# Causal mask as a TensorE product on the scores, softmax read from the bank, early scores, and a pool product beside the mixer's attention

## The reference, cut to what matters

```python
s = jnp.einsum('bqhd,bkhd->bhqk', q_blk, k, preferred_element_type=jnp.float32) * scale
if cum_t is not None:                      # forgetting attention (FoX)
    s = s + c_q[..., :, None] - cum_t[:, :, None, :]
s = jnp.where(k_pos[None, :] <= q_pos[:, None], s, NEG_INF)
p = jax.nn.softmax(s, axis=-1).astype(v.dtype)
return jnp.einsum('bhqk,bkhd->bqhd', p, v)
```

## Time and profile before

| | |
|---|---|
| median of 3 runs | 1812.03 us (1811.85 to 1817.65) |
| profiled execution | 1805.45 us, span 1803.7 us |
| busy: PE, DVE, ACT, POOL | 1641.2, 1204.0, 862.6, 56.5 us |
| mean granted TensorE clock | 0.936 of 2.4 GHz |
| chain that ended last | PE 71%, DVE 17%, ACT 5%, DMA 4% |
| layers, mixer, top-k and first table, second table end | to 716, to 917, to 1401, to 1788 us |

### The profile page before, as it was taken

The page is one execution under the profiler, slowest core; times in us unless marked ns, Lnnn a source line. Parts: engine busy times, 40 slices in busy tenths (PEclk is TensorE's granted clock), DMA queues, the critical chain, the costliest instruction groups (busy, mean ns, idle before and its releaser), DMA issues.

```text
span 1803.7 us, 30500 instructions
## 1 busy us (share of the span) xinstructions
PE 1641.2 (91%) x10734; PEld 1411.2 (78%) x10734; DVE 1204.0 (67%) x2585; ACT 862.6 (48%) x1380; POOL 56.5 (3%) x87
## 2 busy tenths in 40 slices
PE   6888898898989787998879999989999999999996
PEld 5666866796767665786769999989999777778885
DVE  3575556645655665544565899978878899975554
ACT  3654354344334553343334666656556344435543
POOL 1020100100000201000000000000000000000000
PEclk9999898899888898896889999999999999999998
DMA  6542452355425543551334445544444444455552
GB/s 232 179 164 105 146 190 91 140 172 178 140 71 177 180 141 143 189 191 66 117 130 174 140 166 183 187 142 161 163 160 145 159 164 163 163 186 192 201 188 93
DMA packets 40469, 282.96 MB, mean 157 GB/s; under 512 B 5297, under 2 KB 5441, under 8 KB 6865
## 3 DMA queue, kind: packets, MB, share of 16 engines
q1 hardware_dynamic: 37136, 267.13, 41.8%
q0 software_dynamic: 3264, 14.94, 2.4%
HBM read 279.94 MB, written 2.12 MB: 156 GB/s over the span
## 4 chain that ended last, share of the span: by engine, by line
PE 71%; DVE 17%; ACT 5%; DMA 4%; issue 2%; POOL 1%; DVEq 0%; ACTq 0%; SPq 0%; POOLq 0%
PE banks L566 19%; PE banks L567 18%; PE banks L568 18%; DVE w_lo L1147 4%; DMA raw<-stream 4%; PE banks L608 3%; PE banks L854 3%; PE banks L656 3%; PE banks L670 2%; ACT w_hi L912 1%; PE banks L628 1%; ACT scratch L977 1%; PE banks L682 1%; PE banks L681 1%; PE banks L680 1%
## 5 line engine op out<-in xcount | busy, mean ns | idle before, releaser
L1147 DVE TENSOR_TENSOR w_lo<-raw,w_hi 128x1024 fp32r<-128x1024 f32 x456 | 560.7, 1232 | 407.0 <-ACT w_hi L912 403.9
L912 ACT ACTIVATE w_hi<-raw 128x1024 fp32r<-128x1024 f32 x456 | 482.2, 1058 | 584.0 <-PE banks L568 501.5
L566 PE MATMUL banks<-w_hi,xT_hi 128*128 128x512 f32 (+2 forms) x1140 | 454.5, 399 | 20.3 <-DVE xT_lo L1179 16.2
L567 PE MATMUL banks<-w_lo,xT_hi 128*128 128x512 f32 (+2 forms) x1140 | 445.1, 390 | 0.0
L568 PE MATMUL banks<-w_hi,xT_lo 128*128 128x512 f32 (+2 forms) x1140 | 444.9, 390 | 0.0
L566 PE MATMUL banks<-xT_hi,w_hi 128*128 128x256 f32 x1360 | 394.5, 290 | 5.2 <-ACT xT_hi L958 1.5
L567 PE MATMUL banks<-xT_lo,w_hi 128*128 128x256 f32 x1360 | 388.4, 286 | 0.0
L568 PE MATMUL banks<-xT_hi,w_lo 128*128 128x256 f32 x1360 | 388.3, 286 | 0.0
L566 PEld LDWEIGHTS banks<-w_hi,xT_hi 128*128 128x128 f32 x1140 | 218.9, 192 | 66.4 <-ACT xT_hi L958 13.0
L566 PEld LDWEIGHTS banks<-xT_hi,w_hi 128*128 128x128 f32 x1360 | 264.9, 195 | 7.2 <-ACT arena L1077 2.6
L567 PEld LDWEIGHTS banks<-xT_lo,w_hi 128*128 128x128 f32 x1360 | 264.7, 195 | 0.0
(11 more groups left out here) (188 smaller groups left out, 1495.7 us busy)
## 6 DMA issues: line engine op xcount, KB each, us to landing
raw<-stream SPq DMA_DIRECT2D x252, 1024.0 KB, 4.8
arena<-ln_in POOLq DMA_DIRECT2D x4, 1024.0 KB, 5.0
arena<-mod_rows POOLq DMA_DIRECT2D x2, 1536.0 KB, 8.8
arena<-g_in POOLq DMA_DIRECT2D x3, 512.0 KB, 7.3
arena<-x_in SPq DMA_DIRECT2D x1, 1024.0 KB, 5.1
arena<-bands_in POOLq DMA_DIRECT2D x1, 1024.0 KB, 5.2
arena<-keys_in POOLq DMA_DIRECT2D x1, 1024.0 KB, 5.0
x_spill<-arena POOLq DMA_DIRECT2D x1, 1024.0 KB, 4.9
```

The lines of the kernel that those rows point to most:

```text
L566: pe.matmul(out, stationary[0], moving[0], start=first, stop=False, **k)
L567: pe.matmul(out, stationary[0], moving[1], start=False, stop=False, **k)
L912: act.activation(w_hi[:, s], raw[:, s // 2, (s % 2) * PIECE:(s % 2 + 1) * PIECE], ACT.Copy).then_inc(piece_hi, 1)
L1147: dve.tensor_tensor(w_lo[:, s], raw[:, s // 2, (s % 2) * PIECE:(s % 2 + 1) * PIECE], w_hi[:, s].bitcast(F32), ALU.subtract).then_inc(piece ...
```

## The change

It has these parts.

1. *Mask and scale.* The queries are scaled when they are evacuated (`scaled`). A bf16 product `ident` x `causal` adds the mask to the own block of each query block in the bank, two per head, in MLA, FoX and the mixer. Maxima and exps read the bank. The bank is given back by the exps (`probs_ready`), and not by L1265, which is gone there; SWA keeps it.
2. *Early scores.* `first_scores` computes two heads before the last gate unit (SWA, FoX, mixer) or before the last two units of query turns (MLA); in the loop scores run one head further ahead. Ada chunk 0 goes to step 0, the others to steps 5 to 13. In MLA keys are turned before queries. In FoX the forget sums are computed before v is evacuated.
3. *Mixer.* The rotation and turns of q and k, the pool mix and the gates are interleaved; the pool products run in eight halves beside the attention (`project_half`).
4. *Stream.* Each chunk is fetched in two transfers of 512 KB, with a semaphore and a buffer release for each half. `kept` (with `ident`) is loaded from POOL's queue. At a layer's start x is evacuated before further splits; a split leaves the end of the layer norm; the silu of c moves to ScalarE's start.

```diff
+                    for half in range(2):
+                        if len(freed) >= 2 * RAW:
+                            sp.wait_ge(*freed[-2 * RAW])
+                        s = len(freed) % (2 * RAW)
+                        sp.dma_start(half_raw(s), stream[n][:, half * PIECE:(half + 1) * PIECE]).then_inc(piece_landed[s], 16)
+                        if use == "split":
+                            split += 1
+                            freed.append((piece_lo, split))
+                        else:
+                            freed.append((ada_used, summed + 1))
+                    summed += use == "sum"
+                    if len(freed) == 2 * RAW:
...
-                    sp.wait_ge(piece_lo, 2 * RAW * turn - 2 * RAW + 2 * s + 2 - 2 * DEPTH * ADA_CHUNKS)
-                    sp.dma_start(raw[:, s], stream[RAW * turn + s]).then_inc(chunk_landed[s], 16)
+                    for half in range(2):
+                        sp.wait_ge(piece_lo, 2 * RAW * turn - 2 * RAW + 2 * s + half + 1 - 2 * DEPTH * ADA_CHUNKS)
+                        sp.dma_start(half_raw(2 * s + half), stream[RAW * turn + s][:, half * PIECE:(half + 1) * PIECE]).then_inc(
+                            piece_landed[2 * s + half], 16)
```

```diff
+            def scores(h, q, k, fox=False, swa=False):
+                g = heads_done[0] + h
+                if swa and h >= 2:
+                    pe.wait_ge(scores_taken, h - 1)
+                elif g >= 2:
+
+                    pe.wait_ge(probs_ready, g - 1)
+                bank = banks[:, 4 + g % 2]
+                qh, kh = q(h), k(h)
+                if fox:
+                    pe.wait_ge(aug_ready, h + 1)
+                for cols, qb, n in (((0, P), 0, P), ((P, 3 * P), 1, 2 * P)):
+                    mm = pe.matmul(bank[:, cols[0]:cols[1]], qh[:, qb * P:(qb + 1) * P], kh[:, 0:n],
+                                   start=(qb == 0), stop=swa, skip_group_check=True)
+                    if fox:
+                        r = HD * (h % 2)
+                        mm = pe.matmul(bank[:, cols[0]:cols[1]], attn["aug"][r:r + 48, h % 2, qb * P:(qb + 1) * P],
+                                       aug[r:r + 48, 1, 0:n], start=False, stop=False, skip_group_check=True)
+                    if not swa:
+                        mm = pe.matmul(bank[:, cols[1] - P:cols[1]], mask[:, 0], mask[:, 1], start=False, stop=True, skip_group_check=True)
+                mm.then_inc(scores_full, 1)
...
+
+            def project_half(unit, k):
+
+                if k == 0:
+                    bank_free(unit)
+                if k % PK == 0:
+                    half_taken[:] = take_piece()
+                for b in range(B):
+                    mm = parts_product(bank_of(unit, b), [x[:, unit.k0 + k, b * P:(b + 1) * P] for x in (xT_hi, xT_lo)],
+                                       [w[:, k % PK] for w in half_taken], k == 0, k == unit.ktiles - 1, skip_group_check=True)
+                if k % PK == PK - 1:
+                    drop_piece(mm)
```

```diff
-                    if i < heads:
-                        scores(i)
-                    if i % 2 == 1 and i // 2 < ada:
-                        ada_chunk(i // 2)
+                    if ada and i == 0:
+                        wait_put(pe, late[:1])
+                        ada_chunk(0)
+                    if beside and i == 2:
+                        wait_put(pe, late)
+                    if i != 1 and max(i + 1, 2) < heads:
+                        scores(max(i + 1, 2), q, k, fox, swa)
+                    if ada and i == 5:
+                        wait_put(pe, late)
+                    if i % 2 == 1 and 2 <= i // 2 <= ada:
+                        ada_chunk(i // 2 - 1)
                     if 1 <= i <= heads:
                         turn_probs(i - 1)
                     if i >= 2:
                         outputs(i - 2)
+                    if 0 <= i - 2 < 4 * len(beside):
+                        project_half(beside[(i - 2) // 4], (i - 2) % 4)
                 heads_done[0] += heads
```

```diff
+                    pe.wait_ge(k_built, l // 3 + 1)
+                    for u, ready in zip(L["kT"], L["kv_up"]):
+                        wait_put(pe, [ready])
+                        turn(u, mla["k"])
                     pe.wait_ge(q_roped, l // 3 + 1)
-                    for u in L["qT"]:
+                    for u in L["qT"][:2]:
                         turn(u, mla["q"])
-                    pe.wait_ge(k_built, l // 3 + 1)
-                    wait_put(pe, L["kv_up"])
-                    for u in L["kT"]:
-                        turn(u, mla["k"])
-                    wait_put(pe, L["qT"] + L["kT"])
-                    attention(HEADS, lambda h: mla["qT"][0:MLA_DK, h], lambda h: mla["kT"][0:MLA_DK, h],
-                              lambda h, b: mla["kv"][:, b, 2 * HD * h + HD:2 * HD * (h + 1)], ada=ADA_CHUNKS)
+                    wait_put(pe, L["kT"] + L["qT"][:1])
+                    pe.wait_ge(mask_ready, 1)
+                    queries, keys = lambda h: mla["qT"][0:MLA_DK, h], lambda h: mla["kT"][0:MLA_DK, h]
+                    first_scores(queries, keys)
+                    for u in L["qT"][2:]:
+                        turn(u, mla["q"])
+                    wait_put(pe, L["qT"][1:2])
+                    attention(HEADS, queries, keys, lambda h, b: mla["kv"][:, b, 2 * HD * h + HD:2 * HD * (h + 1)],
+                              ada=ADA_CHUNKS, late=L["late"])
                     o = mla["o"]
```

```diff
-            for i, u in enumerate(M["u"] + M["q"] + M["k"] + M["v"] + M["gates"]):
+            for i, u in enumerate(M["u"] + M["q"] + M["k"] + M["v"] + M["gates"][:2]):
                 project(u, M["hT"][1:] if i == 0 else ())
+            pe.wait_ge(q_roped, 3)
+            for u in M["qT"]:
+                turn(u, moba["q"])
+            pe.wait_ge(k_built, 3)
+            for u in M["kT"]:
+                turn(u, moba["k"])
...
-            wait_put(pe, [unit])
+            project(M["gates"][2])
+            wait_put(pe, M["qT"] + M["kT"])
+            queries = lambda h: moba["qT"][HD * (h % 2):HD * (h % 2 + 1), h // 2]
+            keys = lambda h: moba["kT"][HD * (h % 2):HD * (h % 2 + 1), h // 2]
+            first_scores(queries, keys)
+            project(M["gates"][3])
+            wait_put(pe, M["diffT"])
...
+            attention(MOBA_HEADS, queries, keys, lambda h, b: moba["v"][:, b, HD * h:HD * (h + 1)], late=M["mixT"], beside=M["pool"])
             pe.wait_ge(out_taken, heads_done[0])
             for u in M["oT"]:
                 turn(u, moba["o"])
-            wait_put(pe, M["mixT"])
-            for u in M["pool"]:
-                project(u)
             wait_put(pe, M["oT"])
```

```diff
-                            ins = act.activation(probs[:, g % 2, lo:hi], s_sb[:, g % 2, lo:hi], ACT.Exp,
+                            masked = s_sb[:, g % 2, lo:hi] if kind == "swa" else banks[:, 4 + g % 2, lo:hi]
...
+                    if i == 2 and last_gate is not None:
+                        split_ahead(last_gate.pieces_done)
+                    if i == 0 and mix is not None:
+                        evacuate_only(mix)
+                        split_ahead(mix.pieces_done)
+                    if beside and i >= 4 and i % 2 == 0:
+
+                        split_ahead(before + i // 2 - 1)
                 heads_done[0] += heads
```

```diff
                     if kind == "swa":
-
+                        if g >= 2:
+
+                            dve.wait_ge(probs_ready, g - 1)
                         slope = float(2.0 ** (-8.0 * (h + 1) / HEADS))
-                        ins = dve.scalar_tensor_tensor(out=s_sb[:, g % 2], in0=const("dist"), scalar=-slope, in1=raw_scores,
-                                                       op0=ALU.mult, op1=ALU.add)
-                    else:
-                        ins = dve.scalar_tensor_tensor(out=s_sb[:, g % 2], in0=raw_scores, scalar=scale, in1=const("causal"),
-                                                       op0=ALU.mult, op1=ALU.add)
-                    ins.then_inc(scores_taken, 1)
-                    dve.wait_ge(scores_taken, g + 1)
-                    dve.tensor_reduce(neg_max[:, g % 4, 0:1], s_sb[:, g % 2, 0:P], AX.X, ALU.max, negate=True)
-                    b = dve.tensor_reduce(neg_max[:, g % 4, 1:2], s_sb[:, g % 2, P:3 * P], AX.X, ALU.max, negate=True)
+                        dve.scalar_tensor_tensor(out=s_sb[:, g % 2], in0=const("dist"), scalar=-slope, in1=masked,
+                                                 op0=ALU.mult, op1=ALU.add).then_inc(scores_taken, 1)
+                        dve.wait_ge(scores_taken, h + 1)
+                        masked = s_sb[:, g % 2]
+                    elif g >= 4:
+
+                        dve.wait_ge(probs_ready, g - 3)
+                    dve.tensor_reduce(neg_max[:, g % 4, 0:1], masked[:, 0:P], AX.X, ALU.max, negate=True)
+                    b = dve.tensor_reduce(neg_max[:, g % 4, 1:2], masked[:, P:3 * P], AX.X, ALU.max, negate=True)
                     if kind == "swa":
```

(42 more changed lines are left out.)

210 lines of the change are left out of this document (114 added, 96 removed).

## The result

The changed kernel took 1817.12 us (median of 20 runs, 1807.56 to 1826.17) against 1812.69 for the kernel before in the same rounds: a ratio of 1.004, with a 95% interval of 1.0022 to 1.0058. It is 0.4% slower. The program has a faster and a slower state, and a ratio here compares the executions in the faster one, so it need not be the quotient of the two medians. 1760 had been forecast, with a range of 1735 to 1792 and 0.95 for faster. The profiled execution took 1822.84 us around a span of 1821.0.

The account below looks back on a forecast made before the run. TensorE's idle time (136 us) and reduced clock (0.89) in the first 990 us were taken as what can be gained. Terms summed to 51.7 us: 1753.8 for the profiled execution, about 1760 for a median, range 1735 to 1792.

Parts of the forecast that it names:

- FoX, the step that failed: FoX attention: forget sums earlier, scores one head ahead, loop starting at full clock; -3.6 us (+4 to -10).
- by the same chain: Head loop: exponentials, scores, turns to division, division, maxima; 4.4 us for two MLA heads, 5.4 in FoX, without ada.
- The mask products: MLA, FoX, mixer: 112 bf16 products at 0.055 us each, 6 us within the loops; 5 to 13 in all.
- rival A: Head loops get longer, as scores wait behind exponentials and mask products or bank reads cost more: 1778 us; A or B 0.16.
- First MLA layer: Earlier first product (-6.5 us), earlier latent turn (-3) and the attention up to the turn of o (-4.6).
- gives back nothing and costs nothing: MLA head loop: keeps the lead of 4.1 us at head 0; turn of o at 147.9 us against 152.5.
- Second MLA layer: Latent turn -3 us, attention -6 us, as its turns had run at half clock.
- SWA: SWA attention: scores one head ahead and ada chunks until head 12 shorten the loop and half-clock stretch; -3 us (+1 to -8).
- Mixer: Mixer's attention: interleaved turns, pool products beside the heads, clock above 0.9; -20 us (-8 to -25).
- Layer edges and stream: Layer starts: a split leaves the front of x's evacuation, -2 us in all; stream halves in the table stages, nothing.
- Rival C: Table stages: halves served one by one make the stream the bound, 84 us more, 1844 us; chance 0.03.
- rival B: Clock stays low after idle gaps; mixer gives 8 us, FoX and SWA nothing: 1780 us; A or B 0.16.

Follow-up runs that it names:

- run 1: Changed kernel with FoX's forget row written two heads ahead, behind the maxima: median 1801.8 us against 1814.44 for the kernel before.
- run 2: Kernel before with FoX's forget row written one step later, behind a division: 1854.48 us, ratio 1.022.
- run 5: run 1's kernel with the mixer's pool products behind the attention again: 1808.5 us, ratio 0.9925 to the kernel before.
- run 10: run 9's kernel with the mask on TensorE, products together: 1763.74 us; then also probability turns ahead of scores: 1811.51 us.
- run 4: run 1's kernel with the weights' stream in whole 1 MB chunks again: 1778.36 us, ratio 0.984 to the kernel before.
- Run 7: Kernel before with the mask part alone (mask products, queries scaled at evacuation, reads from the bank): 1809.25 us, ratio 0.9999.
- run 6: run 1's kernel with both mask products of a head behind its last product of keys: 1773.43 us, ratio 0.980 to the kernel before.
- run 11: run 9's kernel with the stream in whole 1 MB chunks again: 1757.22 us, ratio 0.975 to the kernel before.
- run 3: run 1's kernel with the mask back on VectorE instead of mask products: 1761.6 us, ratio 0.970 to the kernel before.
- run 9: run 3's kernel with VectorE's division one step later: 1746.96 us, ratio 0.964 to the kernel before.
- run 8: Kernel before with the mask part alone, the first query block's mask product left out: 1799.78 us, ratio 0.9934.

## Why the prediction was wrong, point by point

- **FoX, the step that failed.** I wrote that its loop would take 5.4 us a pair, 6.5 with ada, "by the same chain", 48.7 us from first turns to turn of o. It took 96.1 (448.74 to 544.81). Of the new order I followed one wait, scores behind exponentials, and not the other that TensorE's scores have, for the forget row. The row came a whole step too late for scores one head ahead. Runs 1 and 2 show it from both sides: 16.3 us of idle time gone with the row in time, and 41.4 us more with the row late in the kernel before. Clock and mask products made up the rest, and runs 1, 5 and 10 show that it can also fall with the row in time. It is no rival of mine: the 0.03 for slower stood on the stream. Without it the same sum ends 46.9 us lower (43.3 + 3.6), at 1776 for the profiled execution. The length of a pair was too short as well. With the row in time and full clock (run 4) two heads took 5.94 us, and 7.08 with one ada chunk, 0.5 to 0.6 over my 5.4 and 6.5: about as much as the mask products cost above their price (next point).
- **The mask products.** 0.055 each was right for MLA (0.06) and wrong for FoX: 0.21 between products of 64 and 48 rows. With 64 at 0.06, 32 at 0.21 and the mixer's 16 at the same, which no row was read for, they come to 14 us, just above my upper bound of 13. TensorE was the limit in FoX already before (steps of 2.60), so there they lengthen the loop, as rival A had it. Run 7: the mask part by itself is worth nothing. Reading from the bank costs nothing, as I took it: in the first MLA attention the exponentials of 128 and 256 columns take 0.37 and 0.47 us from the bank after, 0.40 and 0.49 from SBUF before, and the maxima 0.28 and 0.41 in both.
- **First MLA layer,** +0.1 against -14.1. The start gave 5.1 (19.72 to 14.59; 6.5 forecast). The latent turn came 5.6 earlier, nearly all of it from the start, not 3 more; that a half takes 3.6 us to land, not 2.7, is the likely reason, but was not tested. The first exponentials came 7.0 us earlier (112.48 to 105.50). Then the clock fell, and the loop took 41.4 us for 35.1: all was given back by the turn of o (152.59, before 152.49). At full clock, in run 4, the loop is as long as before (35.5), as I said: "gives back nothing and costs nothing". The pairs were right: 5.3 us with ada and 4.2 to 4.5 without, in the second MLA loop, at full clock, for 5.4 and 4.4. I had argued from the first MLA loop before, which kept its clock.
- **Second MLA layer** -6.4 for -9, **SWA** -5.7 for -3: within their bounds.
- **Mixer,** -10.6 for -20. The mechanism held (run 5), the clock not above 0.9 but 0.86, and the eight heads took 28.2 us from first to last exponentials (859.91 to 888.11), where I had 23.1 for their steps. With the clock of run 6, 24.7.
- **Layer edges and stream** -3.5 for -2, and halves 0: run 11 puts the halves at 6 us between the two profiles, 10 between the medians and 19 by the ratios. The landing of a half was mis-sized, 3.6 for 2.7: the rate of a half is 146 GB/s and not my 194, a third below the 218 of a whole chunk. The Trainium skill, "DMA: Bandwidth & Descriptors", section Bandwidth, tells to batch to 1 MiB or more. The trace agrees that whole chunks move more for each us of waiting (1024 KB in 4.8 us, 512 KB in 3.6), and not that batching pays here: the earlier half is worth more. Rival C fell.
- **The clock, rival B,** took about 10 us where I had weighed it (6 in the first MLA attention, 3.5 in the mixer's), and of FoX's 43 the part that is neither idle time nor mask products, some 20 (43.3 less 16.3 and 6.7, an estimate).

Why the clock of one stretch falls in one kernel or execution and not in the next is not settled: between FoX's exponentials run 1 was at half clock for 65 us, run 5 with the same code there for 51, run 3 for 17, and run 4 not at all.

The fastest version found is run 9: both kernels are beaten, the one before by 3.6%.

## What to carry to other kernels

When an operation is moved a step ahead, list every semaphore that it waits for, and see for each producer what stands in front of it in its own engine's order; a small producer behind a division that waits for the end of the step closes a loop through both engines. Work that leaves a half-idle engine for the one that sets the pace must be priced between the very neighbours that it will have; and where it can stand last among products of its own shape, put it there. Divisions, and all else that nothing waits for, belong behind what the next head needs.

## What the runs showed of the hardware that was not expected

- A bf16 product of 128 rows and columns costs TensorE 0.06 us among products of 96 and 128 rows at full clock. Between products of 48 and 64 rows it costs 0.36, and behind the last of them 0.06 (1.51, 1.63 and 1.93 us for a head's scores with none, both behind, and one of each; leaving out the one between shortens a step by 0.35, run 8).
- TensorE was granted 1.2 GHz through stretches in which the profile has it busy without a gap, 44.00 of 44 us in run 1. The Trainium skill, "TensorE: Matmul & The Clock Gate", Part 1, section "What's actually happening", gives a busy array the full 2.4 GHz and an idle one half of it; these rows do not agree, with the reservation that the ends of products are modelled in the profile.
- A transfer of 512 KB took 3.6 us from issue to landing as one of a stream of them, and 2.7 in the two with which the kernel ends, in the same profile; those write the output, and I had taken their time for a read.
